# Half of a query chunk multiplied inside the first stage, and two more weight tiles used unsplit

## The chip, the cores and the metric

The kernel runs on one core of a Trainium2 chip. The metric is the device time of one launch in microseconds (us). Five engines work side by side and meet only at semaphores: TensorE (PE), VectorE (DVE), ScalarE (ACT), GpSimd (POOL) and SyncE (SP). POOL and SP here do little but issue DMAs.

## The reference, cut to what matters

Two layers of a decoder trunk, 256 tokens, 2048 channels, all in float32:

```
cond = silu(c)
for each layer:
    shift1, scale1, gate1, shift2, scale2, gate2 = cond @ w_ada + b_ada      # 6 vectors of 2048
    h    = rmsnorm(x) * (1 + scale1) + shift1
    proj = h @ w_in            # 1024 pooling u, 1024 queries q, 6 x 256 keys and values, 24 gate logits
    a    = causal pooling of u over windows 2, 4, 8, 16, mixed by w_pool
    o    = sparse attention: compressed, selected and sliding branches
    x    = x + gate1 * (concat[a, o] @ w_out)
    h2   = rmsnorm(x) * (1 + scale2) + shift2
    x    = x + gate2 * ((silu(gate) * up) @ w_down)
```

`w_ada` alone is 2048 x 12288 per layer. It is read as 384 halves of 512 KB, each of which gives half of the sum for 128 values of one vector.

## The kernel before

**Weights.** All other weights come as a stream of tiles of 128 x 2048 floats (1 MB; a few are smaller) in the order of their use. SP loads tile n into `raw[n % 4]`, one of four buffers, when tile n - 4 has been used. In layer 0, tiles 0 to 11 are three 512-column chunks of keys and values, each in four groups of four 128-row steps k. Tiles 12, 15, 17, 18 are query chunk 0 and tiles 20, 22, 23, 25 query chunk 1, each with its groups 0 to 3. Tile 13 holds the gate logits, 14, 16, 19, 21 the compression MLP (`hidden`), 24 its second matrix (`cmp_out`). From tile 26 on come the eight tiles of the pooling projection, then w_out, and from tile 52 the MLP.

**Split and unsplit tiles.** Normally ACT rounds each half of a tile to float32r (`split_hi`, L1241), DVE makes the remainder (`split_lo`, L1651), and PE multiplies three float32r products (`tile`, L652: 24 matmuls of 128x512 a tile). Before tile 26 of layer 0 the tiles are unsplit: PE multiplies the raw float32 tile with the float32 `xT` (`first_chunks` L861, `unsplit` L760: 8 matmuls a tile, each of which the trace shows as two records).

**The first stage of layer 0** (`first_norm`, `first_chunks`) can't start a pair of steps before its scale and shift are there. POOL loads the 64 halves of shift1 and scale1 in order into slots (L546), DVE sums each against `cond` (L1681), ACT then makes the rows h of steps k (L1366), and PE multiplies each pair of steps with all three chunks: 12 matmuls a pair. The last two steps are made one at a time. The 11 slots are the three `ada` buffers and, as long as they hold nothing else, `qT` (2), `kT`, `val`, `uc`, `pT` and `gate` (2).

**After it** DVE goes on with conditioning sums for later vectors, a number for each tile (the table `ROOM`), from a ring of five slots: three `ada` buffers and the two halves of `gate` (L552). Between its sums DVE scales the query heads, makes the keys and the hidden activations, and, from tile 26 on, the remainders. From tile 26 on, four more slots lie in `x_sb`, whose float32 rows are no longer read once the last unsplit tile is through. Each of SP, POOL, DVE, ACT and PE takes its instructions in the order of the program, so a wait holds up all that stands behind it on that engine.

## Time and profile before

| | |
|---|---|
| median of 3 runs | 2160.4 us (2160.2 to 2161.89) |
| profiled execution | 2161.69 us |
| its span | 2159.9 us |
| granted clock over it | 0.995 |
| PE busy | 2124.8 us, 98% |
| DVE, ACT, POOL busy | 1552.1, 984.0, 208.4 us |
| HBM read | 592.18 MB |

The span runs from the first to the last instruction; the 1.8 us beside it lie around the program. Busy shares are means over stages with very different limits, so the stages have to be read one by one.

### The profile page before, as it was taken

To read this page: it belongs to the slowest core of one execution; us is meant where nothing else is said; L and a number is where in the kernel's file an instruction comes from. 1 tells how busy PE (TensorE), PEld (TensorE's weight loads), DVE (VectorE), ACT (ScalarE), POOL (GpSimd) and SP (SyncE) were. 2 spreads that over 40 slices of the span, in tenths; PEclk is the share of its full clock that TensorE was granted. 3 is DMA by queue.
4 is the path that set the end of the run, shared out by engine and by line. 5 is a ranking of instruction groups with operands and counts; after the bars stand their busy time and mean duration, and the time that the engine had idled before them with its cause. 6 is when DMAs were issued, how large, how long until landed. Compare 5 with 4: busy or idle time off the path is not lost.

```text
span 2159.9 us, 25296 instructions
## 1 busy us (share of the span) xinstructions
PE 2124.8 (98%) x9624; PEld 1687.5 (78%) x9624; DVE 1552.1 (72%) x2271; ACT 984.0 (46%) x1515; POOL 208.4 (10%) x392
## 2 busy tenths in 40 slices
PE   7899999999999999999999999999999999999999
PEld 3345888788888888888878788878888888888887
DVE  6767998898688887787877775678755555455555
ACT  2123664744344444443465476475434443344443
POOL 3312122111011111111001100001000000000000
PEclk9999999999999999999999999999999999999999
DMA  9999899899598888888757865468755555555554
GB/s 391 412 393 413 314 341 383 303 349 361 203 340 318 328 320 318 314 317 320 289 205 273 333 242 188 156 230 310 288 215 195 187 186 194 193 191 187 190 192 156
DMA packets 112028, 595.97 MB, mean 276 GB/s; under 512 B 12642, under 2 KB 13090, under 8 KB 65188
## 3 DMA queue, kind: packets, MB, share of 16 engines
q1 hardware_dynamic: 55232, 390.83, 48.4%
q0 software_dynamic: 56384, 203.45, 25.4%
q8 instruction: 76, 1.25, 0.2%
q14 instruction: 44, 0.36, 0.0%
q10 hardware_dynamic: 292, 0.09, 0.0%
HBM read 592.18 MB, written 2.13 MB: 275 GB/s over the span
## 4 chain that ended last, share of the span: by engine, by line
PE 92%; DMA 3%; DVE 2%; issue 2%; ACT 1%; ACTq 0%; DVEq 0%
PE ps L652 80%; PE ps L861 1%; DMA ada<-w_ada 1%; DMA gate<-w_ada 1%; PE ps L1018 1%; PE ps L987 1%; PE ps L1123 1%; DMA kT<-w_ada 1%; PE ps L622 1%; PE ps L621 1%; PE ps L615 1%; PE ps L1064 1%; PE ps L995 1%; PE ps L836 0%; PE ps L790 0%
## 5 line engine op out<-in xcount | busy, mean ns | idle before, releaser
L1651 DVE TENSOR_TENSOR w_lo<-raw,w_hi 128x1024 fp32r<-128x1024 f32 x664 | 799.2, 1223 | 328.3 <-ACT w_hi L1241 327.8
L1241 ACT ACTIVATE w_hi<-raw 128x1024 fp32r<-128x1024 f32 x664 | 694.7, 1058 | 640.7 <-PE ps L652 613.2
L652 PE MATMUL ps<-w_hi,h_hi 128*128 128x512 f32 x1696 | 466.0, 396 | 0.0
L652 PE MATMUL ps<-w_hi,h_lo 128*128 128x512 f32 x1696 | 454.3, 390 | 0.0
L652 PE MATMUL ps<-w_lo,h_hi 128*128 128x512 f32 x1696 | 454.0, 389 | 0.0
L652 PEld LDWEIGHTS ps<-w_hi,h_lo 128*128 128x128 f32 x1696 | 318.3, 188 | 67.6
L652 PEld LDWEIGHTS ps<-w_lo,h_hi 128*128 128x128 f32 x1696 | 318.3, 188 | 67.2
L652 PEld LDWEIGHTS ps<-w_hi,h_hi 128*128 128x128 f32 x1696 | 313.6, 188 | 65.7 <-issue 4.0
L652 PE MATMUL ps<-w_hi,a_hi 128*128 128x512 f32 x848 | 234.4, 398 | 0.0
L652 PE MATMUL ps<-w_hi,a_lo 128*128 128x512 f32 x848 | 227.0, 389 | 0.0
L652 PE MATMUL ps<-w_lo,a_hi 128*128 128x512 f32 x848 | 226.9, 389 | 0.0
L652 PEld LDWEIGHTS ps<-w_hi,a_hi 128*128 128x128 f32 x848 | 157.9, 188 | 36.2 <-issue 4.8
L652 PEld LDWEIGHTS ps<-w_hi,a_lo 128*128 128x128 f32 x848 | 159.2, 188 | 33.6
L652 PEld LDWEIGHTS ps<-w_lo,a_hi 128*128 128x128 f32 x848 | 159.2, 188 | 33.5
L552 POOL DMA_DIRECT2D ada<-w_ada x164 | 86.8, 529 | 769.1 <-DVE half_sum L1681 521.0
L1681 DVE CUSTOM_DVE_ANT_0 ada<-ada,cond,nv 128x1024 f32<-128x1024 f32 x96 | 121.5, 1280 | 19.8 <-DMA k_sb<-const 10.6
L1681 DVE CUSTOM_DVE_ANT_0 ada<-ada,cond,half_sum 128x1024 f32<-128x1024 f32 x86 | 108.8, 1282 | 9.6 <-DMA ada<-w_ada 9.2
L861 PE MATMUL ps<-raw,x_sb 128*128 128x512 f32 x192 | 90.2, 633 | 21.9 <-ACT x_sb L1366 21.9
L1585 ACT ACTIVATE bufa<-ps 128x256 f32<-128x256 f32 x88 | 33.5, 385 | 164.5 <-PE ps L652 162.0
L2135 DVE TENSOR_TENSOR bufb<-bufa,ps 128x256 f32<-128x256 f32 x84 | 33.9, 421 | 89.5 <-ACT bufa L1585 89.2
L861 PEld LDWEIGHTS ps<-raw,x_sb 128*128 128x128 f32 x192 | 38.7, 204 | 72.3 <-issue 59.8
L2045 DVE TENSOR_TENSOR bufa<-ps,gate 128x512 f32<-128x512 f32 x60 | 38.7, 686 | 49.9 <-PE ps L652 46.5
(246 smaller groups left out, 1600.9 us busy)
## 6 DMA issues: line engine op xcount, KB each, us to landing
raw<-stream SPq DMA_DIRECT2D x360, 1024.0 KB, 5.3
ada<-w_ada POOLq DMA_DIRECT2D x182, 512.0 KB, 6.8
qT<-w_ada POOLq DMA_DIRECT2D x52, 512.0 KB, 7.6
uc<-w_ada POOLq DMA_DIRECT2D x29, 512.0 KB, 7.8
kT<-w_ada POOLq DMA_DIRECT2D x26, 512.0 KB, 7.2
val<-w_ada POOLq DMA_DIRECT2D x26, 512.0 KB, 7.5
pT<-w_ada POOLq DMA_DIRECT2D x26, 512.0 KB, 7.5
gate<-w_ada POOLq DMA_DIRECT2D x26, 512.0 KB, 11.7
```

The lines of the kernel that those rows point to most:

```text
L552: pool.dma_start(ada_buf[s], w_ada[q]).then_inc(ada_landed[s].sem, 16)
L615: mm = pe.matmul(bank[:], xh, whi[s][:, k, :], start=begin, stop=False)
L621: pe.matmul(bank[:], xh, wlo[s][:, k, :], start=False, stop=False)
L622: mm = pe.matmul(bank[:], xl, whi[s][:, k, :], start=False, stop=end)
L652: mm = pe.matmul(banks[tok][0][:], rows[2 * a + k][low][:, tok * P:(tok + 1) * P], w[s][:, k, :], start=first and a == 0 and i == 0 and k ...
L861: mm = pe.matmul(bank[:], xT[:, k, tok * P:(tok + 1) * P], raw[t % 4][:, k % 4 * COLS:(k % 4 + 1) * COLS], start=(k == 0), stop=(k == KT - 1))
L1241: act.activation(whi[h % 4][:].rearrange("p k c -> p (k c)"), raw[t % 4][:, a * 1024:(a + 1) * 1024], ACT.Copy).then_inc(hi_ready.sem, 1)
L1585: act.activation(bufa[:, k % 2, tok * 256:(tok + 1) * 256], bank[:, 0:256], ACT.Silu)\
L1651: dve.tensor_tensor(wlo[h % 4][:].rearrange("p k c -> p (k c)"), raw[t % 4][:, a * 1024:(a + 1) * 1024], whi[h % 4][:].rearrange("p k c -> ...
L1681: dve.tensor_tensor_reduce(ada_buf[s], ada_buf[s], cond[:, a * ADA_K:(a + 1) * ADA_K], 1.0, start, ALU.mult, ALU.add, total).then_inc(ada_ ...
L2045: dve.tensor_tensor(buf[:, tok, :], ps[b][:], gate[:, n * 512:(n + 1) * 512], ALU.mult)\
L2135: dve.tensor_tensor(bufb[:, k % 2, tok * 256:(tok + 1) * 256], bufa[:, k % 2, tok * 256:(tok + 1) * 256], ps[b][:, 256:512], ALU.mult).the ...
```

## The change

Two things are done in layer 0; layer 1 only takes its groups of query chunk 1 in another order.

**Part one.** Tiles 22 and 23 now hold groups 0 and 1 of query chunk 1 (steps k = 0 to 7; `Q1_GROUPS` = 2, 0, 1, 3). In layer 0 they don't go through `raw`: SP loads each into the `gate` buffer during the first stage, the first behind tile 5, the second behind tile 8. PE multiplies them in `early_queries`, one before steps 6 and 7, the other before steps 10 and 11, into the banks A and B. ACT copies the two sums to the upper half of `qT` (`q1_part`), and at tile 25 DVE adds them to the rest (`add_parts`), from where ACT takes the squares. As `gate` is lent to the weights, the first stage has nine slots for the halves instead of eleven, and tile 9 and tile 12 wait for 44 and 62 sums (none and 60 before). The window keys move from `qT` to `bufb`.

**Part two.** Tiles 26 and 27, the first two of the pooling projection, are used unsplit (`T_SPLIT` = 28), so ACT and DVE don't split them. The slots in `x_sb` are lent from tile 28 on instead of 26. `ROOM` moves conditioning sums to later tiles: 18 instead of 27 stand ahead of the hidden activations (those of tiles 10 to 22), five fewer up to tile 36, and the two tables are level again at tile 47.

```diff
-UNSPLIT = half_of(T_U0)
-RAW_AFTER = {1: 6, 2: 8, 3: 14, 12: 60}
+T_SPLIT = T_U0 + 2
+UNSPLIT = half_of(T_SPLIT)
+RAW_AFTER = {1: 6, 2: 8, 3: 14, 9: 44, 12: 62}
+Q1_GROUPS, Q1_EARLY, EARLY_BEHIND = (2, 0, 1, 3), (22, 23), (5, 8)
-ADA_RING, ADA_SLOTS = 3, 11
+ADA_RING, ADA_SLOTS, FIRST_SLOTS = 3, 11, 9
-ROOM = ({10: 3, 11: 2, 12: 5, 15: 5, 17: 4, 18: 4, 20: 2, 22: 2, 25: 2, 26: 3, 27: 1, 28: 2, 29: 4, 30: 3,
+ROOM = ({10: 3, 11: 2, 12: 4, 15: 3, 17: 3, 18: 2, 20: 1, 25: 2, 26: 4, 27: 3, 28: 3, 29: 4, 30: 3, 31: 4, 33: 4, 34: 3, 35: 3,
...
         if q < FIRST_HALVES:
-            s = q % ADA_SLOTS
+            s = q % FIRST_SLOTS
...
+            def load_early(i):
+                if i:
+                    sp.wait_ge(q1_used.sem, 1)
+                sp.dma_start(gate[:], flat[Q1_EARLY[i]]).then_inc(q1_landed.sem, 16)
...
+                    if layer == 0 and t + 4 in EARLY_BEHIND:
+                        load_early(EARLY_BEHIND.index(t + 4))
...
+            def early_queries(h):
+                pe.wait_ge(q1_landed.sem, 16 * (h + 1))
+                for tok, (bank, uses) in enumerate(((bank_a, A_USE), (bank_b, B_USE))):
...
+                    for i in range(4):
+                        mm = pe.matmul(bank.tile[:], xT[:, 4 * h + i, tok * P:(tok + 1) * P],
+                                       gate[:, i * COLS:(i + 1) * COLS],
+                                       start=(h == 0 and i == 0), stop=(h == 1 and i == 3))
+                mm.then_inc(q1_used.sem, 1)
...
+            def first_queries():
+                def q0(t):
+                    unsplit(t, chunk(C_Q), T_Q0.index(t), lambda: middle(t))
+                q0(12)
+                gate_logits()
+                kv_turn(1)
+                hidden(0)
+                q0(15)
+                kv_turn(2)
+                hidden(1)
+                q0(17)
+                skip_landed(T_CMP1[2])
+                hidden(2)
+                skip_landed(T_Q0[3])
+                q0(18)
+                hidden(3)
+                unsplit(T_Q1[0], chunk(C_Q + 1), Q1_GROUPS[0], lambda: None, Q1_GROUPS[0])
+                hidden_fold()
+                stage_turn(bank_a, A_USE["q 0"], ST_Q0, 0, 4)
+                stage_turn(bank_b, B_USE["q 0"], ST_Q0 + 1, 1, 4)
+                unsplit(T_Q1[3], chunk(C_Q + 1), Q1_GROUPS[3], lambda: attention_side(25), Q1_GROUPS[0])
+                cmp_out()
...
                 for ks in steps:
+                    if ks[0] in (6, 10):
+                        early_queries((ks[0] - 6) // 4)
...
-                    tile(t, chunk(C_U + i // 4), h_rows(g), g == 0, g == 3, lambda t=t: middle(t))
+                    if layer == 0 and t < T_SPLIT:
+                        unsplit(t, chunk(C_U + i // 4), g, lambda t=t: middle(t))
+                    else:
+                        tile(t, chunk(C_U + i // 4), h_rows(g), g == 0, g == 3, lambda t=t: middle(t))
...
+                act.wait_ge(q1_used.sem, 2)
+                act.wait_ge(ada_summed.sem, QUERIES_FREE)
+                for tok, bank in enumerate((bank_a, bank_b)):
+                    act.activation(q1_part[tok], bank.tile[:], ACT.Copy).then_inc(q1_kept.sem, 1)
...
+            def add_parts():
+                dve.wait_ge(q1_kept.sem, 2)
+                for tok in range(TOKS):
+                    b = chunk_bank(C_Q + 1, tok)
+                    dve.wait_ge(gemm_done.sem, gemm_done.at(here, 2 * half_of(T_Q1[3]) + 2 + tok + 1))
+                    dve.tensor_tensor(bufb[:, tok, :], ps[b][:], q1_part[tok], ALU.add)\
+                        .then_inc(chunk_free[b].sem, 1)
```

**PE, the first stage.** PE's rows around steps 6 and 7, before: `ps0` to `ps4` and `ps7` are the banks of the three chunks and two token halves, and the brackets say which semaphores a row waits for.

```order
L861 MATMUL ps4<-raw1,x_sb 128x512 [waits raw_landed1]
L861 MATMUL ps4<-raw1,x_sb 128x512
L861 MATMUL ps7<-raw1,x_sb 128x512 x2
L861 MATMUL ps0<-raw3,x_sb 128x512 [waits first_h] x2
L861 MATMUL ps1<-raw3,x_sb 128x512 x2
```

The same place of the change; banks A and B are `ps5` and `ps6`.

```order
L933 MATMUL ps4<-raw1,x_sb 128x512 [waits raw_landed1]
L933 MATMUL ps4<-raw1,x_sb 128x512
L933 MATMUL ps7<-raw1,x_sb 128x512 x2
L878 MATMUL ps5<-gate,x_sb 128x512 [waits a_free,q1_landed]
L878 MATMUL ps5<-gate,x_sb 128x512 x3
L878 MATMUL ps6<-gate,x_sb 128x512 [waits b_free]
L878 MATMUL ps6<-gate,x_sb 128x512 x3
L933 MATMUL ps0<-raw3,x_sb 128x512 [waits first_h] x2
```

Eight matmuls now stand ahead of the wait for step 6's rows; eight more stand in the same way ahead of step 10.

**SP, the first stage.** SP's load queue from tile 4 on, before:

```order
L503 DMA raw0<-stream 128x2048 [waits gemm_done]
L503 DMA raw1<-stream 128x2048 [waits gemm_done]
L503 DMA raw2<-stream 128x2048 [waits gemm_done]
L503 DMA raw3<-stream 128x2048 [waits gemm_done]
L503 DMA raw0<-stream 128x2048 [waits gemm_done]
```

And with the change:

```order
L521 DMA raw0<-stream 128x2048 [waits gemm_done]
L521 DMA raw1<-stream 128x2048 [waits gemm_done]
L500 DMA gate<-stream 128x2048
L521 DMA raw2<-stream 128x2048 [waits gemm_done]
L521 DMA raw3<-stream 128x2048 [waits gemm_done]
L521 DMA raw0<-stream 128x2048 [waits gemm_done]
L500 DMA gate<-stream 128x2048 [waits q1_used]
L521 DMA raw1<-stream 128x2048 [waits gemm_done,ada_summed]
```

Two loads of 1 MB have moved from behind tile 21 to behind tiles 5 and 8, ahead of the end of the first stage.

## Rows read from the trace of the kernel before

**Rows 1.** The page: span, busy engines, granted clock in 40 slices.

```profile
span 2159.9 us, 25296 instructions
...
PE 2124.8 (98%) x9624; PEld 1687.5 (78%) x9624; DVE 1552.1 (72%) x2271; ACT 984.0 (46%) x1515; POOL 208.4 (10%) x392
...
PEclk9999999999999999999999999999999999999999
```

**Rows 2.** Windows: length; busy PE, PEld, DVE, ACT, POOL; clock; DMA share; GB/s.

```profile
70.00:97.00 27.00, 22.52 (x48) 9.68 (x48) 20.43 (x35) 3.45 (x6) 8.23 (x16) 0.94 1.02 413
97.00:131.00 34.00, 31.26 (x66) 13.73 (x67) 27.51 (x49) 6.33 (x11) 6.92 (x14) 0.90 0.99 399
131.00:160.00 29.00, 29.00 (x169) 14.66 (x168) 19.11 (x53) 8.98 (x34) 5.81 (x11) 1.00 0.98 389
160.00:180.00 20.00, 20.00 (x106) 9.34 (x106) 12.32 (x29) 3.64 (x19) 3.70 (x7) 1.00 1.02 414
...
235.00:300.00 65.00, 65.00 (x329) 53.64 (x328) 59.01 (x128) 39.97 (x91) 11.02 (x21) 1.00 0.89 333
300.00:340.00 40.00, 40.00 (x196) 32.08 (x195) 37.48 (x66) 23.23 (x46) 11.72 (x18) 1.00 0.95 335
...
378.00:2160.00 1782.00, 1774.35 (x8196) 1460.89 (x8194) 1246.15 (x1666) 835.64 (x1170) 121.11 (x229) 1.00 0.69 254
```

**Rows 3.** PE's timeline, 20 to 240 us: start, length, what; idle before and its releaser.

```profile
33.17 33.34 PE L861 MATMUL ps<-raw,x_sb 128*128 128x512 f32 x72 [11.20 <-ACT x_sb L1366]
71.79 22.52 PE L861 MATMUL ps<-raw,x_sb 128*128 128x512 f32 x48 [5.28 <-ACT x_sb L1366]
99.74 32.48 PE L861 MATMUL ps<-raw,x_sb 128*128 128x512 f32 x68 [5.43 <-ACT x_sb L1366]
132.06 1.04 PE L876 MATMUL ps<-k_sb,qT 128*128 128x128 f32 x8
...
168.08 1.15 PE L929 MATMUL ps<-raw,pT 128*32 128x128 f32 x32
...
184.62 1.07 PE L876 MATMUL ps<-k_sb,bufb 128*128 128x128 f32 x8
185.53 7.03 PE L760 MATMUL ps<-raw,x_sb 128*128 128x512 f32 x16
...
196.78 1.08 PE L953 MATMUL ps<-raw,pcT 128*60 128x128 f32 x8 [0.35 <-DVE pcT L1928]
```

**Rows 4.** ACT's timeline, 20 to 215 us: the rows h of steps 10, 11 and of step 15.

```profile
99.09 1.09 ACT L1366 ACTIVATE x_sb<-x_sb,mod 128x256 f32<-128x256 f32 x2 [15.75 <-DVE mod L1690]
...
126.34 0.60 ACT L1366 ACTIVATE x_sb<-x_sb,mod 128x256 f32<-128x256 f32 x1 [6.93 <-DVE mod L1690]
```

**Rows 5.** DVE's timeline, 20 to 215 us: sums, the first behind the roots, three late ones.

```profile
27.22 1.28 DVE L1681 CUSTOM_DVE_ANT_0 qT<-qT,cond,nv 128x1024 f32<-128x1024 f32 x1
...
28.43 1.28 DVE L1681 CUSTOM_DVE_ANT_0 kT<-kT,cond,nv 128x1024 f32<-128x1024 f32 x1
...
117.22 1.28 DVE L1681 CUSTOM_DVE_ANT_0 qT<-qT,cond,half_sum 128x1024 f32<-128x1024 f32 x1 [2.47 <-DMA qT<-w_ada]
...
124.82 1.28 DVE L1681 CUSTOM_DVE_ANT_0 pT<-pT,cond,half_sum 128x1024 f32<-128x1024 f32 x1 [1.20 <-DMA pT<-w_ada]
...
154.10 1.28 DVE L1681 CUSTOM_DVE_ANT_0 ada<-ada,cond,nv 128x1024 f32<-128x1024 f32 x1 [4.32 <-DMA ada<-w_ada]
```

**Rows 6.** The chain that ended last, 0 to 420 us: a split tile.

```profile
202.15 5.49 PE ps L652 x24
```

**Rows 7.** The tile `raw` on SP, 150 to 170 us: issues and their time to landing.

```profile
L503 SPq DMA_DIRECT2D raw<-stream x5: 327/328/328, 152.7 to 169.3; - x5
...
DMA to landing us min/median/max: 7.9/9.0/11.7
```

**Rows 8.** ACT's timeline, 313 to 319 us: the last step of one head's softmax.

```profile
316.64 0.90 ACT L1406 ACTIVATE bufa<-bufa,fac 128x256 f32<-128x256 f32 x2
```

**Rows 9.** PE's timeline, 311 to 327 us: the transpose that reads that softmax.

```profile
318.56 0.60 PE L995 MATMUL ps<-k_sb,bufa 128*128 128x128 f32 x4
```

More of the change, by code:

```diff
@@ L393, in build @@
         nmax, sums, fac = sb("nmax", [P, 2, 2]), sb("sums", [P, 2, 2]), sb("fac", [P, 2, 2])
+        q1_part = [qT[:, tok, 4:8].rearrange("p h t -> p (h t)") for tok in range(TOKS)]
         ada_buf = [a[:] for a in ada]
@@ L559, in _ @@
                 for t in range(TILES):
-                    if layer == 0 and t == T_U0:
+                    if layer == 0 and t == T_SPLIT:
                         pool.wait_ge(gemm_done.sem, gemm_done.start + 2 * UNSPLIT)
+                        last = T_SPLIT - 1
+                        pool.wait_ge(raw_free[last % 4].sem, raw_free[last % 4].at(here, last // 4 + 1))
                         pool.wait_ge(h_ready.sem, 8)
@@ L746, in first_pair, with unsplit @@
                             block_of(t + i, chunks[i], h_rows(0), True, False, a, tok)
-            def unsplit(t, banks, g, between):
+            def unsplit(t, banks, g, between, first=0):
                 loaded(t)
@@ L754, in unsplit @@
                         bank, free, value = banks[tok]
-                        if g == 0 and a == 0:
+                        if g == first and a == 0:
                             pe.wait_ge(free, value)
@@ L761, in unsplit @@
                                            raw[t % 4][:, (2 * a + k) * COLS:(2 * a + k + 1) * COLS],
[L762 to L763 removed]
+                                           start=(kt == 4 * first), stop=(kt == KT - 1))
+                        if t == T_Q1[3] and (a, tok) == (0, 0):
+                            mm.then_inc(gemm_done.sem, 9)
+                        elif a == 0 or g == 3:
                             mm.then_inc(gemm_done.sem, 1)
@@ L885, in kv_turn @@
                         pe.wait_ge(chunk_free[b].sem, chunk_free[b].at(here, C_KV // 2 + 1))
+                        if here.layer == 0:
+                            pe.wait_ge(q1_kept.sem, 2)
                         stage_turn(bank, uses["kv 0"], None, tok, 4, qT[:, tok].rearrange("p h t -> p (h t)"))
@@ L932, in hidden @@
                 if piece < 3:
-                    mm.then_inc(raw_free[t % 4].sem, 1)
+                    mm.then_inc(raw_free[t % 4].sem, 2 if here.layer == 0 and piece == 2 else 1)
                 else:
@@ L1169, in _ @@
                     norm(1, T_KV, chunks)
-                for i, t in enumerate((*T_Q0, *T_Q1)):
+                if layer == 0:
+                    first_queries()
+                for i, t in enumerate((*T_Q0, *T_Q1) if layer else ()):
                     if t == 23:
@@ L1176, in _ @@
                     g = i % 4
-                    if layer == 0:
-                        unsplit(t, chunk(C_Q + i // 4), g, lambda t=t: middle(t))
-                    else:
-                        tile(t, chunk(C_Q + i // 4), h_rows(g), g == 0, g == 3, lambda t=t: middle(t))
+                    tile(t, chunk(C_Q + i // 4), h_rows(g if i < 4 else Q1_GROUPS[g]), g == 0, g == 3,
+                         lambda t=t: middle(t))
                     if t == 12:
@@ L1625, in _ @@
                 for t, nxt in zip(ATT_SPLIT, ATT_SPLIT[1:]):
-                    period(t, nxt if layer or nxt >= T_U0 else None)
+                    period(t, nxt if layer or nxt >= T_SPLIT else None)
                 norm(2, T_MLP)
@@ L1862, in scale_heads @@
                                   ALU.mult).then_inc(stage_ready.sem, 1)
+            def add_parts():
+                dve.wait_ge(q1_kept.sem, 2)
+                for tok in range(TOKS):
+                    b = chunk_bank(C_Q + 1, tok)
+                    dve.wait_ge(gemm_done.sem, gemm_done.at(here, 2 * half_of(T_Q1[3]) + 2 + tok + 1))
+                    dve.tensor_tensor(bufb[:, tok, :], ps[b][:], q1_part[tok], ALU.add)\
+                        .then_inc(chunk_free[b].sem, 1)
             def stage_rstd(c, n):
+                if here.layer == 0 and c == C_Q + 1:
+                    dve.wait_ge(q1_squared.sem, 2)
                 for tok in range(TOKS):
@@ L2092, in period @@
                     silu_hidden()
+                if t == 25 and here.layer == 0:
+                    add_parts()
                 if t == 25:
@@ L2184, in _ @@
                 for t, nxt in zip(ATT_SPLIT, ATT_SPLIT[1:]):
-                    period(t, nxt if layer or nxt >= T_U0 else None)
+                    period(t, nxt if layer or nxt >= T_SPLIT else None)
                 norm(2, T_MLP)
@@ L2216, in layer_stream @@
     for first in (1024, 1536, 0, 512):
-        chunk(w_in, first, every)
+        chunk(w_in, first, [4 * g + i for g in Q1_GROUPS for i in range(4)] if first == 1536 else every)
     out[T_GL].reshape(P, -1, BLK)[:, :KT, :24] = w_in[:, 3584:].reshape(KT, P, 24).transpose(1, 0, 2)
```

46 lines of the change are left out of this document (31 added, 15 removed).

## The prediction, made before the run

> **What bounds the kernel now.** I read the page first. PE is busy for 98% of the span and its clock is full in nearly every slice [rows 1], so from the middle of layer 0 on a PE instruction removed is time won, and nothing else is. The windows say where that does not hold [rows 2]. From 378 us to the end PE is busy for 1774.35 of 1782 us, and the change touches nothing there; all of it must be decided before 378 us. In that part there are three stretches.
>
> The first stage, up to about 134 us. Here the DMA engines are full (share 1.02 and 0.99, 413 and 399 GB/s [rows 2]) and PE waits three times, 11.20, 5.28 and 5.43 us, each time for rows h of ACT [rows 3], which wait for DVE's sums, which wait for their halves [rows 4, 5]. The stage is bound by the bytes that stand ahead of its last half.
>
> From 134 to 202 us PE is busy all the time but for 0.35 us, at 196.78 [rows 3]. DMA is full as well (0.98 and 1.02), and DVE is busy for only 19.11 of 29 and 12.32 of 20 us [rows 2], because it waits for halves, 4.32 us at 154.10 [rows 5]. The 0.35 us is DVE's hidden activations coming late behind such sums. So PE sets the time here, with DMA and DVE close behind.
>
> From 202 to 378 us PE is busy without a gap, DVE for 59.01 of 65 and 37.48 of 40 us, DMA 0.89 and 0.95 [rows 2]. PE is the bound, with a little room on the others.
>
> **What the change does to each.** (a) Taken out of PE's stream behind the first stage: tiles 22 and 23. An unsplit tile takes 7.03 us [rows 3], so -14.1 us.
>
> (b) Tiles 26 and 27 become unsplit. A split tile takes 5.49 us for its 24 matmuls [rows 6], an unsplit one 7.03, so PE pays 2 x 1.54 = +3.1 us. What goes is on DVE and ACT (four halves each, 1.2 us on DVE), which are not the bound, so I count it at nothing; it makes room for the sums that are moved.
>
> (c) The same 16 matmuls in the first stage. At 7.03 us per eight they don't fit whole into the waits of 5.28 and 5.43 us. But the rows h come later too, because of (d). Steps 6 and 7 start at 71.79 before. I put the delay of their half at 4.5 us (one tile of 2.5 us, see (d), and 2 us of lost slots), so at 76.3. The first group of eight ends at 66.5 + 7.0 = 73.5 and is hidden. Steps 6 to 9 are 48 records of 7.03 / 16 = 0.44 us, 21.1 us, to 97.4; the second eight end at 104.4; the rows of step 10 come at 99.74 + 4.5 = 104.2. So they are hidden also, by waits that (d) keeps open. PE could then start step 15, 60 records on, at 104.4 + 26.4 = 130.8. Its rows come later than that, so DMA sets the end. If that cover were gone, the two groups would cost 14.1 us less the waits of 10.7.
>
> (d) DMA in the first stage. Two more loads of 1,048,576 bytes at 413 GB/s [rows 2] are 5.1 us. The lost slots come on top: with nine instead of eleven, two halves fewer are under way when DVE turns to its roots, and the next slot is freed by the sum of 27.22, at 28.4 [rows 5]. Two halves are 2 x 524,288 bytes, 2.5 us, which is the most that the engines can stand idle then; the least is nothing. I take 2.0, since no other load but one tile is asked for at that moment. Against this, tile 12 now waits for 62 sums: in the old trace the last half of the stage comes 1.20 us late beside it [rows 5], and I take those 1.2 back. Together the last half, and with it the rows of step 15, come 5.1 + 2.0 - 1.2 = 5.9 us later: from 126.34 + 0.60 = 126.9 [rows 4] to 132.8. PE began step 15 four matmuls ahead of 132.06, at 128.5 [rows 3], so the rows had 1.6 us in hand. The stage ends 5.9 - 1.6 = 4.3 us later; with a little for tile 9, whose wait for 44 sums puts its bytes ahead of the rows of step 12, I take +4.5. The bounds are +2.3 (no lost slots; PE's own path gives the same, 130.8 against 128.5) and +7.6 (the slots' 2.5 us whole, nothing back and nothing in hand).
>
> The Trainium skill ("DMA: Bandwidth & Descriptors", section "Issuing engines are not separate DMA queues") says that DMAs of SP and POOL run on the same 16 engines and interleave. That speaks against the change: SP's two loads would be free on a queue of their own and are paid in full by that rule, +5.1 instead of 0. The trace agrees: a half that meets a tile is 2.47 us late [rows 5], the 2.5 us of 1 MB.
>
> (e) DVE's wait at 196.78 for late sums: nine fewer sums stand ahead of it, so -0.35 us.
>
> (f) New waits behind the stage. PE now reaches each tile sooner, while SP still asks for a tile only when its buffer is free. Three loads get tight. Tile 19 is asked for when tile 15 is done and needed right behind tile 17, no longer behind 18 also: two short groups and a tile, 0.5 + 1.1 + 7.0 = 8.6 us (a `hidden` group has 1.15 us, a pair of transposes half of 1.07 [rows 3]). Tile 21 is asked for at the end of tile 17 and needed 1.1 + 7.0 = 8.1 us later. Tile 25 takes the buffer of tile 21, so it is asked for behind `hidden(3)` and needed one tile and the fold and transposes later, 7.0 + 1.3 us, less some 0.8 for ACT to pass the buffer on: 7.5 us. Landing takes 7.9, 9.0 and 11.7 us (least, median, most) in this stretch [rows 7]. But the halves that compete are nine fewer. I take +0.8 us for the three, from 0 to 4. Behind a wait of PE for a tile stands all of PE.
>
> (g) The slot `ada0` is now the one that the last half of the stage uses, so the first half of the next ring is asked for only when that is summed, and four more stand behind it on POOL. DVE has no deadline there for some 10 us: nothing.
>
> (h) Adding the parts, two more instructions on DVE before `take_cmp`, and ACT's copies and squares: their product is read by PE first in the middle of tile 28, some 20 us on. Nothing.
>
> (i) The sums moved behind tile 36, five of 1.2 us, 6.0 us of DVE in all. DVE idles for 2.5 us in 300 to 340 and 6.0 us in 235 to 300 [rows 2]. The nearest deadline is the softmax: ACT ends at 317.54 and PE reads it at 318.56, 1.0 us later [rows 8, 9]. One extra sum between can exceed that by 0.2 us. I take +0.3, between 0 and 3.5 (6.0 less 2.5).
>
> Sum: -14.1 + 3.1 + 4.5 - 0.4 + 0.8 + 0.3 = -5.8 us. I round its weakest terms up and say -5.4. The sum is made against the profiled execution, 2161.69 us with its span of 2159.9; that lies 1.3 above the median of 2160.4. On the median: 2155.0 us.
>
> **Rivals.** The price of a measured difference: 0.2% is 4.3 us, about what a measurement of this kernel can tell from no change.
>
> A. The forecast, -5.4, own range -3.5 to -7.5: 0.50.
>
> B. The first stage grows by less: the slots don't matter and PE's fuller clock tells. The clock is at 0.94 and 0.90 in the windows where PE starts again after a wait [rows 2]; after the second eight it starts at once. Then (d) is +2.3 and (f) nothing: -5.4 - 2.2 - 0.8 = -8.4, 2152.0. For it: PE's waits are shorter. Against: the last half can't come sooner than its bytes. 0.14.
>
> C. The gain is lost on the way: +7.6 in the first stage, or +2 to +4 at tiles 19, 21 and 25. Both are single waits of the size of the bounds above; each leaves 0 to -3 us, about 2158.5. For it: all tiles of that stretch are asked for one tile ahead. 0.24.
>
> D. Slower, by late tiles alone. If DMA stays as full as before, each of the three tiles may take the longest landing seen, 11.7 us [rows 7]. Against 8.6, 8.1 and 7.5 us of time this is 3.1, 3.6 and 4.2 us, which add up because each load is asked for behind the work that the one before held up: 10.9 instead of 0.8, and 2160.4 - 5.4 + 10.1 = 2165.1. The gain is gone from a mean landing of 10.1 us on (6.2 us over three tiles beyond a mean of 8.07). Against it: fewer halves compete. 0.12.
>
> **Numbers.** Faster by over 0.2% (below 2156.1): most of A, 0.45, and B, 0.14, so 0.59. Within 0.2%: the rest of A and C, 0.29. Slower by over 0.2%: D, 0.12. The range runs from 2151.5 (B) to 2160.5, the far end of C, and leaves D out.
>
> **What the changed profile would show.** The first stage: share of DMA full but for a dip at 28 to 31 us; steps 10 and 11 begin near 104 with hardly a wait, at full clock; the transposes of 132.06 begin at 136 to 138. Unsplit tiles at 7.03 us. Tile 26 begins 8 to 9 us earlier than before and tile 28 some 6, with PE waits for `raw` of about 1 us in sum. From there to 378 us all stands 5 to 6 us earlier, without a new wait for a softmax or a remainder. Wrong would be: a stage that ends later than 140 us, a wait of PE for a raw tile above 3 us, or waits between 290 and 340 us that add up to more than 2 us.

## The result: 0.3% slower, and the profile after

The changed kernel takes 2167.94 us (median of 7 runs, 2164.1 to 2172.18) where the kernel before takes 2161.36 us in the same session (7 runs, 2160.07 to 2162.31). The ratio is 1.0031, with a 95% interval from 1.0021 to 1.0040: slower by 6.6 us, where 5.4 us less were forecast. In a second session (`e15_after_again`, below) it was 1.0029, from 1.0018 to 1.0039. Single runs of the changed kernel lie 8 and 10 us apart; those of the kernel before lie 2.2 us apart beside the first of them. The profiled execution took 2169.08 us with a span of 2167.3 us, 7.4 more than the span of before [rows 1].

The page of the changed kernel, span, busy engines and clock:

```profile
span 2167.3 us, 25262 instructions
...
PE 2126.2 (98%) x9608; PEld 1684.1 (78%) x9608; DVE 1549.0 (71%) x2269; ACT 980.5 (45%) x1511; POOL 208.4 (10%) x392
```

PE has 16 instructions fewer, as planned, and is busy 1.4 us more: its share tells nothing of where 7.4 us went. The windows do, beside [rows 2] (length; busy PE, PEld, DVE, ACT, POOL; clock; DMA share; GB/s):

```profile
70.00:97.00 27.00, 25.69 (x61) 10.94 (x60) 21.27 (x38) 3.45 (x6) 8.46 (x16) 1.00 1.02 413
97.00:131.00 34.00, 27.02 (x60) 11.74 (x59) 26.23 (x44) 4.04 (x7) 6.34 (x12) 0.90 0.93 373
131.00:160.00 29.00, 29.00 (x137) 14.11 (x136) 22.48 (x59) 11.39 (x37) 7.37 (x14) 1.00 0.96 369
...
300.00:340.00 40.00, 38.93 (x190) 30.73 (x189) 35.30 (x65) 22.85 (x46) 11.00 (x18) 1.00 1.00 356
```

From 97 to 131 us PE is busy for 27.02 us instead of 31.26, and DMA is no longer full. PE's timeline of the changed kernel, 20 to 240 us (L933 is the first stage, L878 the two groups of early query matmuls, L948 transposes, L784 unsplit tiles), shows the place, beside [rows 3]:

```profile
32.57 22.80 PE L933 MATMUL ps<-raw,x_sb 128*128 128x512 f32 x48 [11.21 <-ACT x_sb L1444]
58.20 10.54 PE L933 MATMUL ps<-raw,x_sb 128*128 128x512 f32 x24 [2.83 <-ACT x_sb L1444]
68.58 7.03 PE L878 MATMUL ps<-gate,x_sb 128*128 128x512 f32 x16
76.92 21.07 PE L933 MATMUL ps<-raw,x_sb 128*128 128x512 f32 x48 [1.31 <-ACT x_sb L1444]
97.83 7.03 PE L878 MATMUL ps<-gate,x_sb 128*128 128x512 f32 x16
104.69 10.46 PE L933 MATMUL ps<-raw,x_sb 128*128 128x512 f32 x24
122.14 20.67 PE L933 MATMUL ps<-raw,x_sb 128*128 128x512 f32 x44 [6.98 <-ACT x_sb L1444]
142.65 1.04 PE L948 MATMUL ps<-k_sb,qT 128*128 128x128 f32 x8
...
198.42 7.03 PE L784 MATMUL ps<-raw,x_sb 128*128 128x512 f32 x16
...
233.96 1.12 PE L1096 MATMUL ps<-pcT,vcmp 128*128 128x512 f32 x2 [0.67 <-ACT pcT L1639]
```

Both early groups fill waits, and steps 10 and 11 start at 104.69, where 104.4 was forecast. Then comes a wait that was not there before, 6.98 us ahead of steps 12 to 15, and the transposes stand at 142.65 instead of 132.06 [rows 3]: 10.6 us late where 4.5 were counted. The chain of the changed kernel through that wait (100 to 145 us: start, length, what):

```profile
102.10 17.69 DMA ada<-w_ada
119.78 0.02 issue
119.81 1.28 DVE ada L1768
...
121.39 0.61 ACT x_sb L1444
...
122.14 20.67 PE ps L933 x44
```

The half that ends it is number 55 (of 0 to 63), the last that the rows h of steps 12 and 13 need. Before, its sum started at 107.95, 2.41 us behind that of half 53 (DVE's timeline of the kernel before):

```profile
105.54 1.28 DVE L1681 CUSTOM_DVE_ANT_0 gate<-gate,cond,nv 128x1024 f32<-128x1024 f32 x1
...
107.95 1.28 DVE L1681 CUSTOM_DVE_ANT_0 ada<-ada,cond,half_sum 128x1024 f32<-128x1024 f32 x1
```

The same sums in the changed kernel:

```profile
111.95 1.28 DVE L1768 CUSTOM_DVE_ANT_0 pT<-pT,cond,nv 128x1024 f32<-128x1024 f32 x1
...
116.09 1.28 DVE L1768 CUSTOM_DVE_ANT_0 ada<-ada,cond,half_sum 128x1024 f32<-128x1024 f32 x1 [2.85 <-DMA ada<-w_ada]
...
119.81 1.28 DVE L1768 CUSTOM_DVE_ANT_0 ada<-ada,cond,half_sum 128x1024 f32<-128x1024 f32 x1 [2.43 <-DMA ada<-w_ada]
```

Halves 53, 54 and 55: their sums start 4.1 and 3.7 us apart and not back to back (1.28 us is the length of one sum). Two raw tiles were asked for at 108.3 and 111.8 (tiles 10 and 11), and each lands 8.6 to 9.0 us later.

The transposes 10.6 us late, less two tiles of 7.03 us, put tile 26 at 198.42; before, it started at 201.80, 3.4 us later. Behind the two unsplit tiles, at 215.85, the same transpose is 0.9 us ahead of the old kernel's (216.72): they cost PE 2.5 us. At 233.96 us the same instruction as before stands at the same time (233.98), with a wait of 0.67 us for a softmax. At 319.98, where before has 318.56 [rows 9], it is 1.4 us behind, after a wait of 1.07. The rest is lost behind 370 us. First PE's timeline of the changed kernel there, then DVE's, then the rows of the tile `x_sb` (340 to 385 us):

```profile
374.00 0.47 PE L639 MATMUL ps<-w_hi,h_hi 128*128 128x512 f32 x1 [1.73 <-DVE w_lo L1738]
...
384.00 0.41 PE L824 MATMUL ps<-k_sb,bufb 128*128 128x128 f32 x2 [2.69 <-DVE bufb L1872]
...
384.73 0.63 PE L639 MATMUL ps<-w_hi,h_hi 128*128 128x512 f32 x1
```

```profile
370.23 1.28 DVE L1768 CUSTOM_DVE_ANT_0 ada<-ada,cond,nv 128x1024 f32<-128x1024 f32 x1
...
371.43 1.28 DVE L1768 CUSTOM_DVE_ANT_0 val<-val,cond,nv 128x1024 f32<-128x1024 f32 x1
...
380.48 0.69 DVE L1847 TENSOR_TENSOR x_sb<-x_sb,bufa 128x512 f32<-128x512 f32 x1 [2.30 <-DMA x_sb<-x]
```

```profile
L605 POOL DMA_DIRECT2D x_sb<-x x2: 1249/1253/1257, 341.9 to 353.4; - x2
...
DMA to landing us min/median/max: 18.2/22.6/27.0
```

Two sums stand ahead of a remainder that PE needs (1.73 us), and the fourth load that adds x, asked for at 353.4 and 27.0 us under way, holds DVE and then PE (2.69 us). Before, it was asked for at 347.3, landed after 23.0 us, and the same transposes stood at 377.52, 6.5 us sooner (PE's timeline of the kernel before):

```profile
377.52 0.41 PE L797 MATMUL ps<-k_sb,bufb 128*128 128x128 f32 x2
```

With matmuls at 0.63 instead of 0.39 us behind the wait, the distance is 7.4 us at 411 us and stays so. So the account of the loss is: +10.6 at the first stage, -14.1 for the two tiles, +2.5 for the unsplit ones, and some 8.4 us of waits for a softmax, a remainder and x, with what follows them, between 206 and 390 us.

### The profile page after: what moved, and what is told of

Read it like the earlier page. It is cut to its first block, busy times and chain, and to the rows that moved or that the text cites. A ratio compares the mean times of both kernels' runs of the same rounds, so it can differ in the third digit from the quotient of the medians.

```text
span 2167.3 us, 25262 instructions
## 1 busy us (share of the span) xinstructions
PE 2126.2 (98%) x9608; PEld 1684.1 (78%) x9608; DVE 1549.0 (71%) x2269; ACT 980.5 (45%) x1511; POOL 208.4 (10%) x392
## 3 DMA queue, kind: packets, MB, share of 16 engines
HBM read 592.18 MB, written 2.13 MB: 274 GB/s over the span
## 4 chain that ended last, share of the span: by engine, by line
PE 87%; DMA 6%; DVE 4%; issue 2%; ACT 1%; SPq 0%; POOL 0%; DVEq 0%; ACTq 0%
PE ps L676 75%; PE ps L784 3%; DMA ada<-w_ada 2%; DMA x_sb<-x 1%; PE ps L933 1%; DVE w_lo L1738 1%; PE ps L1197 1%; DMA raw<-stream 1%; PE ps L1092 1%; DMA uc<-w_ada 1%; DVE ada L1768 1%; PE ps L1061 1%; PE ps L646 1%; PE ps L645 1%; PE ps L639 1%
## 5 line engine op out<-in xcount | busy, mean ns | idle before, releaser
L676 PE MATMUL ps<-w_hi,h_hi 128*128 128x512 f32 x1680 | 461.2, 396 | 0.0
L1768 DVE CUSTOM_DVE_ANT_0 ada<-ada,cond,half_sum 128x1024 f32<-128x1024 f32 x93 | 117.3, 1280 | 13.2 <-DMA ada<-w_ada 12.8
L933 PE MATMUL ps<-raw,x_sb 128*128 128x512 f32 x192 | 87.4, 614 | 22.3 <-ACT x_sb L1444 22.3
L933 PEld LDWEIGHTS ps<-raw,x_sb 128*128 128x128 f32 x192 | 37.4, 198 | 71.0 <-issue 68.2
```

The costliest lines, as they stand in the source:

```text
L676: mm = pe.matmul(banks[tok][0][:], rows[2 * a + k][low][:, tok * P:(tok + 1) * P], w[s][:, k, :], start=first and a == 0 and i == 0 and k ...
L933: mm = pe.matmul(bank[:], xT[:, k, tok * P:(tok + 1) * P], raw[t % 4][:, k % 4 * COLS:(k % 4 + 1) * COLS], start=(k == 0), stop=(k == KT - 1))
L1768: dve.tensor_tensor_reduce(ada_buf[s], ada_buf[s], cond[:, a * ADA_K:(a + 1) * ADA_K], 1.0, start, ALU.mult, ALU.add, total).then_inc(ada_ ...
```

## The experiments

All times are compared with the kernel before in the same session (2160.6 to 2161.0 us); 5 to 11 runs each. "The changed kernel" is at 2167.9, and what a run "won" is the difference of the two medians. The changed kernel scatters, so a single gain of 3 to 4 us is not sure to the microsecond: by the ratios the gains of `e1_tiles_held`, `e2_tile9_free`, `e3_x_earlier` and `e4_both` are 2.6, 3.7, 3.0 and 4.8 us, and only the interval of the last lies clear of the changed kernel's 1.0021 to 1.0040.

**The first stage: `e1_tiles_held`, `e2_tile9_free`.**

```diff
-RAW_AFTER = {1: 6, 2: 8, 3: 14, 9: 44, 12: 62}
+RAW_AFTER = {1: 6, 2: 8, 3: 14, 9: 44, 10: 54, 11: 55, 12: 62}
```

> The changed kernel, with the loads of raw tiles 10 and 11 held until 54 and 55 sums are done. Theory 1 (two tiles of 2.5 us each overtake the halves of steps 12 and 13): half 55 lands near 115 us instead of 119.78, PE starts steps 12 to 15 near 116.5 us instead of 122.14, the first transposes stand at 137 to 139 us instead of 142.65, and the kernel ends 4 to 5 us below the changed one, near 2163.5. Rival (the last half of the stage sets its end, in whatever order the bytes come): transposes stay within 1 us of 142.65, the time within 1 us of 2167.9.

Measured: 2164.38 us, ratio 1.0019 (1.0010 to 1.0028), so 3.6 us won. Half 55 starts its sum at 114.26, step 12 starts at 116.59, the transposes stand at 138.22. The theory's places hold, its gain is a little short: PE now waits 2.08 us for tile 11, and three tiles behind the stage come late by 0.16, 0.25 and 0.47 us.

```diff
-RAW_AFTER = {1: 6, 2: 8, 3: 14, 9: 44, 12: 62}
+RAW_AFTER = {1: 6, 2: 8, 3: 14, 12: 62}
```

> The changed kernel with raw tile 9 not held until 44 sums, and tile 12 held until 60 instead of 62. Theory 1 (the bytes ahead of half 55 are the same in either order): half 47 lands 2 to 3 us later than 101.76, half 55 within 1 us of 119.78, steps 12 to 15 start within 1 us of 122.14, the time within 1 us of 2167.9. Rival (tile 9's wait puts its bytes ahead of the rows of step 12): half 55 2.5 us sooner and the stage with it, near 2165.5.

The kernel that ran still holds tile 12 until 62 sums (it was asked for at 128.8, behind the sum of half 61), so tile 9 is its only difference. Measured: 2163.79 us, 1.0014 (1.0004 to 1.0023). My theory missed. Half 47 came 1.9 us later, close to what I said, but half 55 started its sum at 114.47, 5.3 us sooner, more than the rival said, and the transposes stand at 136.13. The bytes ahead of half 55 were not the same: PE reached the point that asks for tile 10 at 109.6 instead of 108.3, with half 53 summed a little sooner, and I read this as enough for half 55 to slip in ahead. PE's timeline of `e2_tile9_free`:

```profile
116.80 19.49 PE L933 MATMUL ps<-raw,x_sb 128*128 128x512 f32 x44 [0.37 <-ACT x_sb L1444]
...
138.72 7.03 PE L784 MATMUL ps<-raw,x_sb 128*128 128x512 f32 x16
```

All profiles with early loads; "ahead by" is how long before the sum of half 53 tile 10 is asked for:

```
kernel              tile 9 held  tile 10 asked  sum of 53  ahead by  sum of 55  transposes
changed kernel      yes          108.3          111.95      3.6      119.81     142.65
e15_after_again     yes          109.0          112.56      3.6      119.17     142.73
e3_x_earlier        yes          109.4          113.03      3.6      119.97     143.81
e2_tile9_free       no           109.6          111.67      2.1      114.47     136.13
e13_table_half      no           110.1          112.10      2.0      114.61     136.22
e14_three_unsplit   no           110.1          112.12      2.0      114.62     136.42
e10_order_and_x     no           111.1          113.12      2.0      115.63     137.23
e9_table_eased      no           110.8          112.79      2.0      115.34     137.91
e5_split_at_26      yes          112.5          113.81      1.3      116.22     138.68
e16_half_and_three  no           112.7          113.96      1.3      116.37     138.91
e1_tiles_held       yes          113.0          111.71     -1.3      114.26     138.22
e4_both             yes          114.1          112.75     -1.3      115.16     139.25
```

`e5_split_at_26` has the first stage of the changed kernel, word for word. Its PE happened to wait 6.56 us at 62 us and was later with everything, and so its tile 10 was asked for only 1.3 us ahead of that sum, and its stage ended 4 us sooner. With 3.6 us ahead the halves 54 and 55 are late each time, with 2.1 or less never: a race, decided by 1.5 us. The old kernel stands at -1.0 (106.5 against 105.54). The two tiles hold up halves in every profile; on the early side it is later ones, such as 56 and 57 in `e2_tile9_free` (118.23 and 121.56), whose rows PE needs later. That tiles 10 and 11 do it is shown by `e1_tiles_held`, which holds only them. Where the line lies between 2.1 and 3.6 us rests on one profile of each kernel; all three late ones also hold tile 9, and `e5_split_at_26` is the only one that holds it, leaves tiles 10 and 11 free and is early.

**The fourth load of x: `e3_x_earlier`, and both edits: `e4_both`.**

```diff
-X_AT = (40, 42, 44, 46)
+X_AT = (40, 42, 44, 45)
```

> The changed kernel, with the fourth adding load of x asked for at tile 45, ahead of its three halves, instead of at tile 46. Theory 1 (the 6 us between 372 and 389 us are the load's lateness): it is issued near 348.6 us instead of 353.42, lands near 370 instead of 380.39, DVE doesn't wait for it, PE's 2.69 us wait at 384.00 and the slow matmuls behind it go, about -4 us, near 2164; 1.73 us of wait for w_lo at 374.00 stays. Rival (DVE's sums are what makes norm 2 late, the load only comes last beside them): less than 1 us won.

Measured: 2164.97 us, 1.0017 (1.0008 to 1.0026), 3.0 us won; the load was asked for at 349.7, 22.8 us under way, DVE doesn't wait for it, and PE's wait of 2.69 us is 0.5. (This profile has the late first stage again.)

> The changed kernel with both earlier edits: raw tiles 10 and 11 held until 54 and 55 sums, the fourth adding load of x asked for at tile 45. Theory (two separate losses): they add, -3.6 and -3.0 us, near 2161.3; transposes near 138 us, the load of x asked for near 345 us and landed near 368, ahead of DVE. Rival (the time won in the first stage was lost at the load of x, so both edits win the same microseconds): 2163.5 to 2164.5.

Measured: 2162.64 us, 1.0009 (1.0000 to 1.0018), 5.3 us won of the 6.6 that the sum of the two gives. The load was asked for at 345.6 and landed at 368.8, the transposes stand at 139.25, and PE's wait of 2.69 us is 0.44: the trace has both losses gone at once. The time lies between the theory (2161.3) and the rival (from 2163.5), so that they don't share a part is not shown.

**Slots and table in the old kernel: `e6_nine_slots`, `e8_room_alone`, `e12_slots_and_table`, `e11_table_x_earlier`.** Here the first stage is the old one, without early loads.

```diff
-ADA_RING, ADA_SLOTS = 3, 11
+ADA_RING, ADA_SLOTS, FIRST_SLOTS = 3, 11, 9
...
-            s = q % ADA_SLOTS
+            s = q % FIRST_SLOTS
```

> The kernel before, with nine instead of eleven slots for the halves of the first stage, no other edit. By the prediction's (d) the stage ends 2.0 us later (0 to 2.5) and its (g), the next ring asked for only behind the last sum, costs nothing: transposes near 134 us instead of 132.06, the time near 2163.4. Rival 1 (slots cost nothing): 2161.4. Rival 2 (the price of (g) is real): more than 3 us in all, most of it behind the stage.

Measured: 2168.4 us, 1.0032 (1.0020 to 1.0045), 7.4 us lost. The transposes stand at 132.10, as before. Rival 2 holds. PE's timeline of `e6_nine_slots`, its waits behind the stage:

```profile
145.87 3.70 PE L760 MATMUL ps<-raw,x_sb 128*128 128x512 f32 x8 [0.62 <-DMA raw<-stream]
...
186.89 1.23 PE L876 MATMUL ps<-k_sb,bufb 128*128 128x128 f32 x8 [1.32 <-DVE bufb L1861]
...
200.45 1.08 PE L953 MATMUL ps<-raw,pcT 128*60 128x128 f32 x8 [1.59 <-DVE pcT L1928]
```

And the chain of the same kernel (120 to 202 us) that leads to the last of them:

```profile
125.29 1.28 DVE ada L1681
...
126.88 1.04 POOL ada L552 x2
127.92 6.20 DMA ada<-w_ada
...
184.41 9.75 DMA gate<-w_ada
...
199.92 0.48 DVE pcT L1928 x2
200.45 1.08 PE ps L953 x8
```

POOL asks for the next halves only behind the sum of half 63, at 126.88 instead of 109.54, and they stay late, half after half, up to the hidden activations at 200 us. (This profile is of the run with the lowest time, 2165.31 us; it shows 3.6 of the 7.4 us, and where the rest goes is not shown.)

```diff
-ROOM = ({10: 3, 11: 2, 12: 5, 15: 5, 17: 4, 18: 4, 20: 2, 22: 2, 25: 2, 26: 3, 27: 1, 28: 2, ...
+ROOM = ({10: 3, 11: 2, 12: 4, 15: 3, 17: 3, 18: 2, 20: 1, 25: 2, 26: 4, 27: 3, 28: 3, ...
...
```

> The kernel before, with only the table of sums by tile (ROOM of layer 0) of the changed one: five sums fewer up to tile 37, five more behind. Theory 1 (the moved sums make the fourth adding load of x late): it is issued near 350 us instead of 347.34, lands at 373 to 378 instead of 370.35 where DVE asks for it at 374.0, and the kernel is 1 to 4 us slower, 2162.4 to 2165.4. Rival (the table is harmless, it was the later end of the first stage that put the load late): within 0.5 us of 2161.4.

Measured: 2167.34 us, 1.0029 (1.0018 to 1.0040), 6.3 us lost: more than I allowed, and nearly the whole loss of the changed kernel, in a kernel with nothing else changed. The load of x is late as expected (asked for at 353.0, landed at 379.1), but DVE didn't wait for it. PE's timeline of `e8_room_alone`:

```profile
221.24 0.66 PE L876 MATMUL ps<-k_sb,bufb 128*128 128x128 f32 x4 [0.75 <-DVE nmax L1984]
...
225.16 0.44 PE L995 MATMUL ps<-k_sb,bufa 128*128 128x128 f32 x2 [0.48 <-ACT qT L1286]
...
236.21 1.12 PE L1022 MATMUL ps<-pcT,vcmp 128*128 128x512 f32 x2 [1.06 <-ACT pcT L1552]
...
321.33 0.63 PE L995 MATMUL ps<-k_sb,bufa 128*128 128x128 f32 x4 [0.28 <-ACT bufa L1406]
...
375.27 0.47 PE L615 MATMUL ps<-w_hi,h_hi 128*128 128x512 f32 x1 [1.73 <-DVE w_lo L1651]
```

I read this as the sums moved into tiles 26 to 28 making the softmax late (2.3 us), and those moved behind tile 37 the waits at 321 and 375 us (2.0 us). With 0.48 us at 383.02 that is 4.8 of the 6.3 us; the rest is in no wait of this list.

> The kernel before with the changed table of sums (2167.3 us), and the fourth adding load of x at tile 45. Theory (the table costs 6.3 us, of which the load of x is the smaller part, since PE's waits of 2.3 us at 221 to 236 us and 1.73 us at 375 us are for DVE and ACT): 1 to 2 us won, 2165.3 to 2166.3. Rival (the load of x is nearly all of the table's price): 2162.5 or less.

The edit is that of `e3_x_earlier`, on top of the table. Measured: 2167.32 us, 1.0029 (1.0018 to 1.0041): nothing won, against both of my numbers. That fits the row that I had passed over: no DVE wait for the load in `e8_room_alone`. In these profiles DVE waits for the load of x only together with unsplit tiles 26 and 27 (2.13 us in `e7_part_two`, and 0.98 us in the second profile of the changed kernel, `e15_after_again`); with them split again (`e5_split_at_26`) it doesn't.

> The kernel before with nine slots in the first stage and the changed table of sums as well. Slots alone gave 2168.4, the table alone 2167.3. Theory (the table answers to the slots: it takes sums away from where nine slots make them late, so the two pay for the same lateness): 2167 to 2169, without the waits of 1.32 and 1.59 us at 187 and 200 us. Rival (two independent prices): 2173 or more.

The edits of `e6_nine_slots` and `e8_room_alone` together. Measured: 2171.22 us, 1.0046 (1.0033 to 1.0058): between the two numbers. The waits of 1.32 and 1.59 us are gone, as the theory has it, and the table's own (0.76, 0.48, 1.01, 0.90 and 1.76 us) are all there. The table answers to the slots at 187 and 200 us, and costs more than it gives back. Nine slots on top of the table still cost 3.9 us; the profiles show 1.9 of them, 1.3 of which are there by 208 us.

**Part two: `e7_part_two`, `e5_split_at_26`.**

```diff
+T_SPLIT = T_U0 + 2
...
-                    tile(t, chunk(C_U + i // 4), h_rows(g), g == 0, g == 3, lambda t=t: middle(t))
+                    if layer == 0 and t < T_SPLIT:
+                        unsplit(t, chunk(C_U + i // 4), g, lambda t=t: middle(t))
+                    else:
+                        tile(t, chunk(C_U + i // 4), h_rows(g), g == 0, g == 3, lambda t=t: middle(t))
```

> The kernel before with part two alone: tiles 26 and 27 unsplit, slots of x lent two tiles on, the changed table of sums; first stage as before. The table alone gave 2167.3. Theory 1 (unsplit costs PE 3.1 us, and DVE's four remainders fewer take away the waits of 0.75, 0.48 and 1.06 us between 221 and 236): near 2168. Rival 1 (PE's price in full): 2170.4. Rival 2 (the relief of DVE repays more than it costs): 2166 or less.

Measured: 2169.03 us, 1.0036 (1.0023 to 1.0049), 1.7 us above the table alone. The times can't tell theory 1 from rival 1 (the intervals are 1.0023 to 1.0049 here and 1.0018 to 1.0040 there); the waits speak for theory 1: the three of 221 to 236 us, 2.3 us, are gone. A wait of 2.55 us at 384.30 came in their place, behind the load of x.

```diff
-T_SPLIT = T_U0 + 2
+T_SPLIT = T_U0
```

> The changed kernel with tiles 26 and 27 split again and the slots of x lent at tile 26, T_SPLIT = T_U0, the table of sums left as it is. By the prediction's (b) PE wins 2 x 1.54 = 3.1 us: near 2164.8, tile 28 3.1 us sooner. Rival (DVE and the late halves bound the stretch from 200 to 236 us; four more remainders of 1.2 us on DVE eat it): less than 1 us won, with waits of PE for ACT or DVE before 236 us that add up to 2 us or more.

Measured: 2170.11 us, 1.0045 (1.0033 to 1.0058): 2.2 us slower than the changed kernel. The rival has its waits (4.85, 0.52, 0.75 and 0.50 us before 236 us), but it allowed only for less of a gain, and they cost more than the 3.1 us. The first of them, and what stands behind it on ACT, in `e5_split_at_26`:

```profile
200.75 0.66 PE L1069 MATMUL ps<-k_sb,bufa 128*128 128x128 f32 x2 [4.85 <-ACT bufa L1488]
```

```profile
197.25 1.06 ACT L1318 ACTIVATE w_hi<-raw 128x1024 fp32r<-128x1024 f32 x1 [8.80 <-DMA raw<-stream]
```

Tile 26 lands at 197.2. ACT and DVE wait for it to split it, and the softmax's small steps are queued behind it on both engines (198.2 to 199.9). Unsplit, the tile is behind nobody: PE alone needs it.

**Putting it together: `e10_order_and_x`, `e9_table_eased`, `e13_table_half`, `e14_three_unsplit`, `e16_half_and_three`, and the changed kernel again.**

```diff
-RAW_AFTER = {1: 6, 2: 8, 3: 14, 9: 44, 12: 62}
+RAW_AFTER = {1: 6, 2: 8, 3: 14, 10: 51, 11: 54, 12: 60}
...
-X_AT = (40, 42, 44, 46)
+X_AT = (40, 42, 44, 45)
```

> The changed kernel with tile 9 not held, raw tiles 10 and 11 held until 51 and 54 sums, tile 12 until 60, and the fourth adding load of x at tile 45. Theory (a race of tiles 10 and 11 against halves 54 and 55, and the load of x, make the loss and the scatter of the changed kernel): half 55 lands by 115 us, transposes at 136 to 138.5, no wait for the load of x, 2160 to 2162 us, and all single runs within 4 us. Rival (a third cause scatters it): single runs again 7 to 8 us apart, or a median above 2163.

Measured: 2161.46 us, 1.0005 (0.9996 to 1.0013); 11 runs from 2160.11 to 2164.23. As expected, and 6.5 us below the changed kernel: two tables of numbers gave back what the change had lost, and nothing of what it should win. In its profile the stage ends 5.2 us late instead of 4.5, PE waits 2.0 us for tiles (0.43, 0.67 and 0.85) instead of 0.8, and 2.7 us (0.65 at 231, 1.06 at 317, 0.51 at 369 and 0.44 at 377 us) for DVE and ACT, where the forecast had 0.3. PE's timeline of `e10_order_and_x`:

```profile
107.32 30.08 PE L933 MATMUL ps<-raw,x_sb 128*128 128x512 f32 x68 [1.14 <-ACT x_sb L1444]
137.23 1.04 PE L948 MATMUL ps<-k_sb,qT 128*128 128x128 f32 x8
...
150.81 3.70 PE L784 MATMUL ps<-raw,x_sb 128*128 128x512 f32 x8 [0.43 <-DMA raw<-stream]
...
186.28 3.70 PE L784 MATMUL ps<-raw,x_sb 128*128 128x512 f32 x8 [0.85 <-DMA raw<-stream]
```

> The kernel e10_order_and_x, with four sums of the table moved forward: one each from tiles 40, 42, 45 and 47 to tiles 17, 18, 20 and 25. Theory (five sums too many behind tile 36 cost 1 us at 317 us and 1.2 us at 371 us): both waits under 0.4 us, 1.5 to 2 us less than e10_order_and_x. Rival (no room ahead either, with nine slots and DMA full to 180 us): PE waits for DVE or ACT near 186 or 196 us by 1 us or more, and the time is the same or longer.

Measured: 2165.35 us, 1.0019 (1.0010 to 1.0028): 3.9 us worse, against the theory. The waits at 317 and 369 us are gone as it says, but in `e9_table_eased` there is a new one:

```profile
217.33 0.66 PE L1069 MATMUL ps<-k_sb,bufa 128*128 128x128 f32 x2 [2.95 <-ACT bufa L1488]
```

Its chain is a half under way for 10.25 us that lands at 211.07, its sum, DVE's roots and the softmax: too early a sum holds what is queued behind it. Another part are tiles: PE waits 1.55 us at 152.60 and 1.27 us at 178.16 for them. The rival had the right cause and the wrong place.

> The kernel e10_order_and_x, with two sums moved forward only: from tiles 40 and 47 to tiles 15 and 17. Theory (the wait of 2.95 us at 217 us in e9_table_eased came from the sums at tiles 20 and 25; ahead of them DVE has room): PE's waits of 1.06 us at 317 us and 0.51 us at 369 us shrink, no new wait above 0.5 us at 180 to 236 us, 2160 to 2161. Rival (every sum moved ahead of 236 us becomes a wait for DVE or ACT there): 2163 or more.

Measured: 2159.72 us, 0.9994 (0.9985 to 1.0002). As expected: two sums find room at tiles 15 and 17, and the waits at 317 and 369 us are gone. PE still waits for tiles (0.59, 0.62 and 0.80 us).

> The kernel e10_order_and_x, with tile 28 unsplit too, T_SPLIT = T_U0 + 3. PE pays 1.54 us, DVE is freed of two remainders of 1.2 us, the slots of x are lent one tile later. Theory (after two unsplit tiles DVE is no longer the bound there): 1 to 2 us longer, 2162.5 to 2163.5. Rival (DVE still bounds the stretch from 200 to 320 us): the waits of 0.65 us at 231 us and 1.06 us at 317 us go, 2161 or less.

Measured: 2159.57 us, 0.9995 (0.9986 to 1.0003): the rival holds. 1.9 us less than `e10_order_and_x`, though by the prediction's price PE has 1.54 us more to do; the wait at 231 is gone and that at 317 us is 0.30.

> The kernel e10_order_and_x with both: two sums moved forward from tiles 40 and 47 to tiles 15 and 17, and tile 28 unsplit too. Theory (each of the two alone took away nearly all waits of PE for DVE and ACT behind 200 us, so both remove the same waits and the second only adds its 1.54 us or its 0.3 us): 2158.8 to 2160.5, no clear gain over 2159.6. Rival (their gains of 1.7 and 1.9 us add): 2157.9 or less.

Measured: 2160.73 us, 0.9999 (0.9990 to 1.0008), 0.2 above the theory's numbers: the two don't add. No version stands clearly below the kernel before; the best two are 0.05% and 0.06% below it, within what can be told.

> The changed kernel once more, unchanged, for its scatter. Theory (tiles 10 and 11 race halves 54 and 55): single runs spread over 6 us or more, median 2166.5 to 2168.5; in the profiled run the issue of tile 10 and the landing of half 55 go together, near 108 us and 119.8 us, or behind 111 us and near 115 us. Rival (the scatter has another source): half 55 lands near 119.8 us whenever tile 10 is asked for.

Measured: 2167.52 us, 8 runs from 2160.47 to 2170.77. The profile has tile 10 at 109.0 and half 55's sum at 119.17, as the theory's first pair. The same code shows other sizes behind 370 us here: the remainder costs 0.77 us instead of 1.73, the load of x 1.37 instead of 2.69. Versions in which both the race and the load of x are settled lie within 2.5 to 4.3 us; those with one of the two left have runs 6.5 to 7.1 us apart. So I put the scatter down to both. The five runs of `e5_split_at_26`, with neither settled, are only 4.0 us apart, and that each long run is one that lost the race was not shown, since only one run of each kernel is profiled.

## Why the prediction was wrong, point by point

(a) Two tiles out of PE's stream, -14.1 us: right. 10.6 us late at the transposes became 3.4 us early at tile 26, so nothing was lost between 143 and 198 us.

(b) Unsplit at 7.03 us: right. The price on PE was 2.5 instead of 3.1 us. That what goes on DVE and ACT counts "at nothing" was wrong, on the other side from the result. Taken with the prediction's 1.54 us a tile, `e5_split_at_26` has 5.3 us for two tiles (2.2 and 3.1) and `e14_three_unsplit` 3.4 us for one (1.9 and 1.54). `e7_part_two` has 1.4 us for two, with an uncertainty at least as large.

(c) 16 matmuls hidden: right, to 0.3 us.

(d) is the first step that failed. The last half landed 5.7 us later, 130.53 against 124.79, for 5.9; but that this fits is luck in part, since the 2.0 us for lost slots in it are 0.0 in `e6_nine_slots` (the last half lands at 124.6, the stage ends at 132.10). That the stage ends by its last half was wrong: the end was set by half 55, 12 us late. I had moved all halves by the same bytes and left their order alone. But tiles 10 and 11 are asked for by PE's progress (106.5 before, 108.3 after), the halves by DVE's (half 55 at 95.27 before, 102.10 after). Tile 10 moved by 1.8 us and half 55 by 6.8, so the tiles came in front of a half that they had followed. Half 53 is 6.4 us late; from it to half 55 the two tiles, 5.1 us by their bytes, add 5.4 us. The PE work behind half 55 (20.67 us) then sets the end. `e1_tiles_held` and the table of twelve profiles show it. The term that was mis-sized most is the "little for tile 9", 0.2 us: without its wait for 44 sums (`e2_tile9_free`) the transposes stand at 136.13, 4.1 us late and near the forecast of 4.5, with it at 142.65. Its bytes don't do this. With the wait the halves before 48 come sooner, PE starts steps 10 and 11 sooner, and tile 10 is asked for sooner and wins the race.

(e) Right: no wait at 196.70.

(f) +0.8 us for late tiles: none in the changed kernel, since the stage ended so late. Where it ends in time, the waits for tiles are 2.0 us (`e10_order_and_x`, `e13_table_half`) and once 2.8 (`e9_table_eased`), within the bounds.

(g) "DVE has no deadline there for some 10 us: nothing." As a reason this failed: in `e6_nine_slots`, with the old table, the halves asked for behind the last sum are late up to 200 us, and that kernel loses 7.4 us, of which its profile shows 3.6. In the changed kernel, whose table has nine sums fewer there, PE waits for nothing between 143 and 206 us; so this step is not where its time went, unless through the table that the slots had made necessary.

(h) Adding the parts: nothing, as far as any trace shows.

(i) is the second step that failed, as a mis-sized term: +0.3 us (0 to 3.5) for the moved sums, where `e8_room_alone` measures 6.3 in the old kernel. In the changed one the waits at 234, 320, 374 and 384 us are 6.2 us, and the half clock behind the last adds 0.9. I looked only at the softmax up to 340 us. The sums moved into tiles 26 to 28 cost 2.3 us there, and behind 370 us stand a remainder (1.73 us) and the load of x (2.69 us), which I had not looked at: I had written that "all of it must be decided before 378 us", and most of it was decided at 374 to 390: the same matmul is 1.65 us late at 369.27 us, another 7.4 at 411. How much of this is the table's and how much that of the unsplit tiles, with which DVE comes to the load of x sooner, is open.

Read wrongly, with no weight in the sum: from 202 to 378 us PE was not quite "without a gap"; it waited 0.38 us at 208.24.

The rivals: D ended on the right side by the wrong mechanism; no tile was late. C named the end of the stage as a place where the gain goes, with +7.6 as its end; 10.6 came. Of the signs that I had named as wrong one came (a stage that ends behind 140 us); the other two, tiles and waits between 290 and 340 us (1.07 us in sum), did not. The profile to expect had no new wait for a softmax or a remainder, and there were three.

The Trainium skill ("DMA: Bandwidth & Descriptors", section "Issuing engines are not separate DMA queues") says that loads from different engines share the 16 DMA engines and interleave. I had used it for the sum of the bytes alone. The trace agrees also within the stage: beside two tiles of SP the sums of POOL's halves started 3.7 to 4.1 us apart and not back to back.

## What to carry to other kernels

When bytes are added to a stage that DMA bounds, list for each transfer what asks for it, and move each by its own clock; then look for pairs that change places, since one deadline ahead of the last one can set the end. When slots are taken away, follow the ring past the stage, to the next engine that waits for a sum, and price that. And when a queue's small works are moved "where there is room", test the table alone: here it cost 6.3 us in the old kernel, nearly as much as the whole change.
